# A whole-model kernel rewritten: small recorded operations, a list scheduler, shared buffer pools, attention in halves of the array

## The reference, cut to what matters

```python
for l in range(DEPTH):
    mod = silu_c @ w_mod[l] + b_mod[l]          # shift, scale, gate: two sets
    hx = modulate(rms_norm(x, norm1_g[l]), sh1, sc1)
    if l % 2 == 0:
        out_x, out_c = even_mixer(hx, hc, ...)   # pooling channels | attention, one output projection
    else:
        out_x = conformer_conv(hx, *conv_args)
    x = x + g1 * out_x
    x = x + g2 * sq_relu_mlp(modulate(rms_norm(x, norm2_g[l]), sh2, sc2), mlp_w1[l], mlp_w2[l])

# attention: 8 query heads, 2 key/value heads of 64; blocks of 128 queries see 256 context keys,
# a sink, and up to 3 blocks of 128 keys (|i - j| <= 128); one softmax over all of them
# conv: a = h @ w_pw1; g = a1 * sigmoid(a2); depthwise conv of width 31;
#       LayerNorm over channels; silu; @ w_pw2
```

## Time and profile before

| what | value |
|---|---|
| three runs | 3942.7, 3958.9, 4101.8 us (median 3958.9) |
| span of the slowest core in the profiled execution | 3916.7 us (all cores 3899.7 to 3916.7) |
| PE busy | 3255.1 us, 83% of the span |
| DVE, ACT, POOL busy | 1877.3, 1261.7, 273.3 us |
| transfers | 247.8 MB written, mean 63 GB/s |

### The profile page before, as it was taken

One profiled execution on the slowest core, in us unless ns is written; L12 is line 12 of the kernel. 1 busy time (PEld: TensorE's weight loads), 2 busy tenths in 40 slices (PEclk: granted clock), 3 DMA queues, 4 the chain that ended last, 5 costly groups with the idle time before them and its releaser, 6 DMA issues.

```text
span 3916.7 us, 44703 instructions; the slowest of 8 cores (3899.7 to 3916.7 us)
## 1 busy us (share of the span) xinstructions
PE 3255.1 (83%) x17961; PEld 1504.3 (38%) x18282; DVE 1877.3 (48%) x2895; ACT 1261.7 (32%) x1889; POOL 273.3 (7%) x287
## 2 busy tenths in 40 slices
PE   2477778999978877799996677789999687799997
PEld 1233334555533333455553233334444233244443
DVE  1233335565631245556663333346656223656666
ACT  4134443111143256211114434441112515621112
POOL 0000000000022000000003100000000400000000
PEclk8688889999988998899998788899999799899998
DMA  9932335544213532544321222235432146122212
GB/s 182 148 52 36 45 46 77 74 60 70 34 22 58 119 89 46 76 66 72 49 38 27 55 49 49 43 55 85 76 62 37 30 90 142 29 43 44 39 27 86
DMA packets 225888, 247.84 MB, mean 63 GB/s; under 512 B 15120, under 2 KB 196752, under 8 KB 225680
## 3 DMA queue, kind: packets, MB, share of 16 engines
q0 software_dynamic: 154160, 170.61, 29.4%
q1 hardware_dynamic: 71520, 74.36, 7.3%
HBM read 397.96 MB, written 17.56 MB: 106 GB/s over the span
## 4 chain that ended last, share of the span: by engine, by line
PE 64%; issue 15%; ACT 7%; DVE 6%; DMA 4%; POOL 2%; another core or an unknown queue 0%; SPq 0%; DVEq 0%; POOLq 0%; ACTq 0%
PE ps L143 64%; DVE ARENA L143 5%; ACT ARENA L143 3%; ACT H L143 3%; POOL TMP L143 2%; DMA ARENA<-w_mod 2%; DMA ARENA<-ropes 1%; DMA wr<-w_in 1%; DVE TMP L143 1%; ACT RST L143 1%; DMA ARENA<-gscr 0%; DVE X L143 0%; POOL ARENA L143 0%; ACT L143 0%
## 5 line engine op out<-in xcount | busy, mean ns | idle before, releaser
L143 PE MATMUL ps<-H,wr 128*128 128x512 bf16 (+1 forms) x6558 | 1432.0, 376 | 66.9 <-ACT ARENA L143 33.9
L143 PE MATMUL ps<-ARENA,wr 128*128 128x512 bf16 (+1 forms) x5085 | 1091.3, 371 | 69.7 <-DVE X L143 62.6
L143 ACT ACTIVATE ARENA<-ps 128x512 f32<-128x512 f32 (+2 forms) x1033 | 565.3, 583 | 1797.7 <-PE ps L143 1765.0
L143 DVE SCALAR_TENSOR_TENSOR X<-ps,MODV,X 128x512 f32<-128x512 f32 (+1 forms) x1296 | 905.7, 719 | 195.0 <-PE ps L143 123.4
L143 PEld LDWEIGHTS ps<-H,wr 128*128 128x128 bf16 x6704 | 665.9, 100 | 800.8 <-issue 73.5
L143 DVE TENSOR_TENSOR ARENA<-ARENA 128x512 bf16<-128x512 f32 (+4 forms) x849 | 527.6, 628 | 907.7 <-ACT ARENA L143 905.2
L143 PEld LDWEIGHTS ps<-ARENA,wr 128*128 128x128 bf16 x5184 | 508.0, 99 | 632.4 <-DVE X L143 84.7
L143 PE MATMUL ps<-ARENA 128*32 128x512 bf16 (+4 forms) x3389 | 419.9, 386 | 244.1 <-DVE ARENA L143 116.7
L143 DVE TENSOR_TENSOR ARENA<-ps,ARENA 128x512 bf16<-128x512 f32 (+5 forms) x300 | 197.5, 671 | 442.1 <-PE ps L143 350.2
L143 PEld LDWEIGHTS ps<-ARENA 128*32 128x32 bf16 (+2 forms) x3410 | 148.2, 102 | 498.3 <-ACT ARENA L143 137.2
L143 ACT ACTIVATE H<-TMP,AB 128x512 bf16<-128x512 f32 (+1 forms) x296 | 210.4, 727 | 106.2 <-POOL TMP L143 54.9
(11 more groups left out here) (41 smaller groups left out, 682.9 us busy)
## 6 DMA issues: line engine op xcount, KB each, us to landing
wr<-w POOLq DMA_DIRECT2D x64, 1024.0 KB, 9.3
ARENA<-w_mod POOLq DMA_DIRECT2D x48, 1024.0 KB, 14.7
ARENA<-gscr SPq DMA_DIRECT2D x256, 135.0 KB, 3.5
wr<-w_in POOLq DMA_DIRECT2D x18, 1024.0 KB, 10.2
wr<-w_out POOLq DMA_DIRECT2D x18, 1024.0 KB, 11.0
wr<-pw POOLq DMA_DIRECT2D x12, 1024.0 KB, 9.6
X<-xT SPq DMA_DIRECT2D x4, 2048.0 KB, 36.5
gscr<-ARENA SPq DMA_DIRECT2D x64, 128.0 KB, 1.7
```

The lines of the kernel that those rows point to most:

```text
L143: ins = getattr(e, it[1])(*it[2], **it[3])
```

## The change

The arithmetic is almost the same; the program around it is new.

- **Recording and scheduling.** Operations are now small objects (`Rec.add`) with an engine, a fixed cost, keys read and written, and virtual buffers. `Rec.schedule` then plays them forward in time and starts on each free engine the ready operation with the lowest number whose buffers fit. What comes out is still one fixed order per engine, made before the program runs. Waits that other waits imply are left out (`_emit_waits`).
- **Pools.** PSUM is a pool of 8 banks, weights a pool of 5 slabs (shared with the modulation slabs), and scratch tiles come from pools that all stages share. H is also the target for queries, attention and pooling outputs.
- **Order of tiles.** Context tile 4 first, then 0 to 3; the first mixer starts when tiles 4 and 0 have their norm and 4 modulation slabs are there. Layer 0's other slabs come later.
- **Attention** (`att`): the two groups' score matmuls go to two halves of the rows into two banks, with one Exp of 128x1024 and one mask for both; the products with V and with ones have 64 columns each and go to two halves of the columns; the denominator is handled for both groups at once. U is computed once per block, together with V.
- **Statistics.** Sums over channels use 32 columns of ones: four chunks go to four column groups of one bank; one more matmul with a constant matrix adds the groups up, after ACT and DVE have split the float32 sum into two bf16 parts (`norm`, `ln`).
- **Convolution.** Sigmoid is replaced by Tanh of half the argument with the factor 0.5 folded into a constant. The norm's multiplication runs on DVE, not on POOL.
- **Packed inputs.** The host lays out weights, X and the output so that each partition's row is contiguous.

```diff
-NSLOT = 4
+NSLOT = 5
...
+    def schedule(self):
...
+                    while h and n < 60:
+                        pr = heap_pop(h)
+                        o = ops[pr[1]]
...
+                        got = fits(o)
+                        if got is None:
+                            tried.append(pr)
+                            continue
+                        pick = (o, got)
+                        break
...
-                            MM(PS[sbk][:, :], KT[gs, m * 128:(m + 1) * 128], Qs[gs, :, nl * 128:(nl + 1) * 128], True, True,
-                               reads=KTk + Qk, writes=[psk(sbk)], last=True)
-                            ACT(P[:, :], PS[sbk][:, :], AF.Exp, [psk(sbk)], Pk, scale=0.125)
...
+                            return [(sc.ap[:, g * 512:(g + 1) * 512].rearrange("p (c q) -> p c q", c=4),
+                                     KT.ap[g * 64:(g + 1) * 64, m * 128:(m + 1) * 128],
+                                     H[t][g * 64:(g + 1) * 64, 0:4, nl * 128:(nl + 1) * 128],
+                                     True, True, [KT.k(m)] + hk(t)[0:4], sc.keys()) for g in range(2)]
...
+                        ACT("Exp", lambda sc=sc, P=P: (P.ap[:, :], sc.ap[:, :], {"scale": 0.125}), sc.keys(), P.keys(), 1024)
...
+                            for g in range(2):
+                                out.append((pnd.ap[g * 64:(g + 1) * 64, 0:512], V.ap[:, m * 128 + g * 64:m * 128 + (g + 1) * 64], P.ap[:, g * 512:(g + 1) * 512],
+                                            first, lst_, [V.k(m)] + P.keys(), pnd.keys()))
+                            for g in range(2):
+                                out.append((pnd.ap[g * 64:(g + 1) * 64, 512:1024], ONE1[:, :], P.ap[:, g * 512:(g + 1) * 512],
+                                            first, lst_, [("one1",)] + P.keys(), pnd.keys()))
...
-                for c in range(8):
-                    MM(PS[pb][:, 0:n], ONES[:, :], H[:, c, t0:t0 + n], c == 0, c == 7,
-                       reads=[("H", ti, c), ("c", "ones")], writes=[psk(pb)], last=(c == 7))
...
+                return [(pa.ap[32 * (c % 4):32 * (c % 4) + 32, 0:n], ONES[:, :], H[t][:, c, :], c < 4, c >= 4,
+                         [("H", t, c), ("ones",)], [pa.k(c % 4)]) for c in range(8)]
```

The sequence in which the mixer of an even layer is recorded, which sets the numbers that the scheduler goes by:

```diff
+            if upd:
+                rest(4)
+            att(0)
+            poolmix(0)
+            proj(2, True)
+            proj_out(wo, 0, l)
+            norm(0, l, 1)
+            att(1)
+            poolmix(1)
+            proj(3, True)
+            proj_out(wo, 1, l)
+            norm(1, l, 1)
+            rest(2)
+            rest(3)
```

More of the change, by code:

```diff
@@ L104, in op, with mm @@
         eng.q.append(("op", meth, args, kw or {}, eng.sem, 1))
+        eng.hist[eng.count] = dict(eng.seen)
         self._record(eng, eng.count, reads, writes)
-    def mm(self, out, lhsT, rhs, start, stop, reads=(), writes=(), last=True):
-        if self.dry:
-            return
+    def mm(self, out, lhsT, rhs, start, stop, reads, writes, last):
         eng = self.E["pe"]
@@ new lines, in DMA, with emit, slab @@
+        def DMA(q, chan, f, reads, writes, nbytes, cost=None, soft=(), bias=0):
+            def emit(Sd):
+                ch = chan() if callable(chan) else chan
+                Sd.dmas(q, Sd.chan(ch), f(), phys(reads), phys(writes))
+            return R.add(q, emit, reads, writes, cost if cost is not None else (1.0 if q == "pool" else 0.08), dma=nbytes, soft=soft, bias=bias)
+        MMC = 0.2157
+        def slab(src, cols=4096):
+            vb = VBuf(wpool, "w", 1, 1, "w")
+            DMA("pool", lambda: "w%d" % vb.slot, lambda: [(vb.ap[:, 0:cols], src)], [], vb.keys(), 128 * cols * 4)
+            return vb
@@ new lines, in poolmix @@
+                    ACT("Identity", lambda pp=pp, g4=g4: (H[t][:, g4, :], pp.ap[:, 0:n], {"scale": vec("pscale", i2 * 4 + g4, i2 * 4 + g4 + 1)}),
+                        pp.keys() + VK, [("H", t, g4)], n, 1)
+            proj(4, upd)
+            proj(0, True)
+            proj(1, True)
+            if pre is not None:
+                pre()
+            wo = [slab(w_out[i2 * 2]), slab(w_out[i2 * 2 + 1])]
+            if pre is not None:
+                for j in range(6, 12):
+                    mod_slab(0, j)
@@ new lines, in build, with pre0 @@
+        norm(4, 0, 0)
+        norm(0, 0, 0)
+        for t in (1, 2, 3):
+            load_x(t, [("modv", 0, 3)])
+            norm(t, 0, 0)
+        def pre0():
+            mod_slab(0, 4)
+            mod_slab(0, 5)
+        for l in range(DEPTH):
+            upd = l < 2
+            tiles = ORD if upd else ORD[1:]
+            if l % 2 == 0:
+                even_mixer(l, upd, pre0 if l == 0 else None)
+            else:
+                conv_mixer(l, tiles)
+            mlp(l, tiles, None)
@@ L979, in build @@
+        order, total, busy = R.schedule()
+        if info is not None:
+            info["order"] = order
+            info["total"] = total
+            info["busy"] = busy
+        Sd = Sched(nc, st)
+        for o in order:
+            for (vb, s_) in o.allocs:
+                vb.slot = s_
+                bind(Sd, vb)
+            o.emit(Sd)
+        for nm, ch in Sd.chans.items():
+            if nm[0] == "o":
+                Sd.E["sp"].q.append(("wait", ch.sem, ch.count))
         with nc.Block() as block:
-            Sreal.flush(block)
+            Sd.flush(block)
```

1681 lines of the change are left out of this document (978 added, 703 removed).

## The result

The changed kernel takes **3304.62 us** (median of 4 runs, 3265.87 to 3584.15) where the kernel before, on the same chip, took 4030.36 (3942.74 to 4422.25). In some runs of either kernel four or all eight cores show a lower clock than in the others and the time is longer, so the ratio is formed from the undisturbed runs (3265.87 and 3266.98 us of the changed kernel): **0.8286, 95% interval 0.8199 to 0.8374**. A second measurement on another chip gave 0.8321 (0.8305 to 0.8337). The forecast was 3195, with a range from 3070 to 3360.

A forecast was written before the change was run, and what follows sets the result against it. It took PE work (3035 us of a 3917 us span) plus 880 us of waiting and slow clock as the bound; 2853 + 20 + 62 + 112 + 71 + 20 + 22 = 3160 span, plus 35 gives 3195 us, range 3070 to 3360.

The forecast's parts named there:

- The count of work: PE's matmuls over the whole program, counted in units of 0.216 us: 3035 us before, 182 us less after, 2853 remaining.
- the clock was priced in attention only: Lower PE clock in attention's half-idle stretches: 1 us per block, 34 us for both layers.
- Convolution's waits: PE waiting in the convolution mixers: 7 us per tile for 8.5 tiles and 11 us at the borders, 71 us.
- Tile changes: 446 changes of tile shape on PE at 0.04 us each, taken as 20 us; upper end 96 us.
- The start: Time before the first mixer matmul: 10.7 MB to load at 173 GB/s, 62 us where 144 were spent; upper end 98.
- ACT over 75% busy in the even mixers: Expected sign in the attention layers: ACT limits there, over 75% busy, with about 1.02 us per Exp.
- The MLPs' ends: Waiting at the borders of all four MLPs: 20 us, where about 200 were lost before.
- The signs: Expected profile marks: clock 0.96 or more, first mixer matmul near 62 us, first MLP matmul near 353, MLP steps unchanged.
- the halves: Rival in attention: matmuls on two halves of the array don't run side by side; about 3265 us, chance 8%.
- the slots: Rival: five shared weight buffers come free late and slabs hold up PE; slower than before, up to 4440 us, chance 2%.
- Better packed than I think: Rival: projections fill attention and the clock stays up, mixer waits fall from 183 to 80; about 3080 us, chance 10%.
- The waits stay: Rival: mixers keep their share of waiting; only work, start and MLP ends are gained; about 3540 us, chance 10%.

The follow-up runs named there:

- The run without halves: Changed kernel with attention's matmuls no longer split over halves of the array (same rows for both groups' scores, 128 columns for values and ones): 3326.8 us at the lowest.
- the run with full statistics: Changed kernel with the norm's statistics by eight matmuls of full 128 columns instead of four column groups, a split and an adding matmul: 3286.19 us.
- The combination with four slots: Changed kernel with padding written late, eleven vectors in one transfer, norm pieces behind Exp and Silu, and four weight buffers instead of five: 3202.34 us median, ratio 0.8159.
- the combination: Changed kernel with padding written late, the eleven vectors in one transfer, and the second norm's pieces behind Exp and Silu: 3222.4 us at the lowest, ratio 0.8217.
- the run in recorded order: Changed kernel with each engine's operations in program order, not the scheduler's, and layer 0's twelve modulation slabs loaded at the start: 4162.35 us at the lowest.
- the packed vectors: Changed kernel with eleven small vectors in one transfer, the first modulation slab held back, and padding recorded later but still scheduled early: 3266.78 us, ratio 0.8323.
- the padding alone: Changed kernel with the zeros padding the convolution's scratch memory written only after layer 0's last modulation values: 3268.08 us at the lowest.

## Why the prediction was right, and where it was off

Against the profiled execution: span 3160 forecast, 3265.4 measured, 105 us short, and the forecast had 81 us too little busy time and 24 too little idle time. The 35 us that I put between the span and the median were right by chance (the median is 39 over the span, the fastest run 0.5).

| term | forecast | measured | from |
|---|---|---|---|
| PE busy | 2907 (2853 + 34 + 20) | 2988 | page |
| of it work at full speed | 2853 | 2837 | 13,151 units, a chunk at 1.73 |
| of it slow clock | 34 | 70 | half of the 139.5 us that PE was busy at 1.2 GHz |
| of it tile changes | 20 | 45 | 446 x 0.10 |
| of it ends before gaps | 0 | 34 | 204 gaps x (0.38 - 0.216) |
| PE idle at the start | 62 | 64 | 73.00 - 9.23 |
| idle in even mixers | 78 | 85 | 55.2 + 30.1 |
| idle in conv mixers | 71 | 110 | 58.4 + 51.5 |
| idle at MLP ends and the end | 42 | 18 | rows of the stages |

The granted clock was at its lower level for 209 us in all (3265.4 x (1 - 0.968) = 104 is half of that), but PE was idle in 70 of them. The last row is a matter of the profile: a matmul before a gap is shown 0.38 us long, one with another behind it takes 0.216.

- **The count of work held.** The matmuls in 73 to 408 us of after, each at its full-speed duration, are 228 us (forecast 231), and the MLPs of the first two layers take 510 and 512 us, eight steps of 63.98. The run without halves shows that their 480 units were really gone; the run with full statistics shows 24 of the 40 us of the norms. A chunk was priced 0.14 us too high, 10 us in all.
- **The step that failed: the clock was priced in attention only.** I gave 1 us to a block, 34 in all. At 1.2 GHz PE was busy for 68 us in the two even mixers and 69 in the two convolution mixers, half of which is lost: 34 us in the even mixers, as forecast, and 35 in convolution, where I priced none, though the earlier trace rows has 0.91 and 0.93 there. What a gap leaves behind is seen in one row: after 7.06 us of waiting, a chunk takes 3.60 us at a granted clock of 0.50 that takes 1.91 in the earlier trace rows.

```profile
1088.61 3.60 PE L155 MATMUL ps<-ARENA 128*32 128x512 bf16 x32 [7.06 <-DMA ARENA<-gscr]
```

- **Convolution's waits were 39 us too low.** I summed ACT's operations against PE's and found ACT at 34 us per tile. That balance leaves out what stands in a queue at the wrong time: the norm's eight pieces, and the chunk loads, for which PE waited 40.4 of the 80.4 us in this group's row:

```profile
L155 PE MATMUL ps<-ARENA 128*32 128x512 bf16 (+3 forms) x3044 | 251.1, 385 | 80.4 <-DMA ARENA<-gscr 40.4
```

In conv 1 the chunk loads took a median of 3.4 us and up to 13. The combination with four slots, made against these two causes, gave 30 us in conv 1 and 11 in conv 3.
- **Tile changes were 0.10 us, not 0.04.** The small remainder that I took from the earlier trace rows came of a chunk priced at 1.87 instead of 1.73 us. The drain of which the Trainium skill speaks (TensorEngine Tiling (Array Packing), Key Properties) fits the trace: 0.10 us at each change, half a matmul, between my two ends.
- **The start: 73 for 62, and for another reason.** I reckoned with bytes alone. The rows below are the start of after (PE's busy time, clock, DMA share, GB/s): the DMA engines are full for 48 us, and then move nothing from 56 to 68, since the next slabs wait for slots that the modulation matmuls hold, and these stand behind norms that came late. In the combination the engines are busy throughout, and it is 55 to 59.

```profile
0.00:48.00 48.00, 0.00 (x0) 1.00 0.96 178
52.00:56.00 4.00, 0.00 (x0) 1.00 0.48 76
56.00:60.00 4.00, 0.61 (x2) 1.00 0.02 2
60.00:64.00 4.00, 1.83 (x6) 1.00 0.00 0
64.00:68.00 4.00, 2.63 (x65) 1.00 0.00 0
```

- **ACT over 75% busy in the even mixers: wrong, and 85 for 78 us of idle time is partly luck.** ACT is busy for 197.11 of 322 us, 61%. The Exp costs what I said (1022 ns), but PE's own part was longer than my 3.2 us per block by slow clock and changes, and I forecast 26 waits of 3.0 us for ACT (by my own terms 6.4 - 3.2 = 3.2, which makes 83). What stands before the score matmuls in 73 to 408 us is far less (count, busy us, mean ns, idle before):

```profile
L155 PE MATMUL ps<-H,ARENA 64*128 64x512 bf16 x164 | 34.1, 434 | 10.3 <-ACT ARENA L155 7.5 <-DVE MODV L155 1.5 <-ACT H L155 0.6
```

In both layers some 31 us of the 85 were waits for an Exp, 10 of them before modulation matmuls. Some 13 were waits for the mask on DVE, which I had put among the work that costs nothing. The others stood before norms, projections and pooling.
- **The MLPs' ends cost nothing** where I gave 20, and the end 18 for 22.
- **The signs.** The mean clock is 0.968 (0.96 or more was forecast). The first MLP matmul comes near 408 us, not 353: 11 us from the start, and 280 us of PE's busy time in layer 0's mixer for 231.
- Of the rivals, the halves are refuted though their time was hit, and the slots are refuted. "Better packed than I think" did not come: the mixers kept 195 us of idle time, not 80. "The waits stay" at 3540 did not come either; the run in recorded order, at 4162, shows how large such waits can get.

## What to carry to other kernels

Once PE is over 90% busy, price each remaining gap twice: its length, and the matmuls behind it at 1.2 GHz; here the second came to some 70 us beside 277 of gaps. When a kernel is built by a list scheduler, look for work that is early because its engine was free, not because anybody waits for it: padding, prefetched slabs and a finished tile's norm each stood before something that PE wanted. Such locks hide one another, so open them together before you judge one worthless: the packed vectors gave nothing while the padding held the start, the padding alone nothing, both together 16 us at the first mixer matmul and 13 in the span.

## What the runs showed of the hardware

- Eleven small transfers of SP (0.5 to 96 KB) landed at 45 us beside software-queue slabs with rows of 8 KB or more, at 18 us beside slabs with rows of 2 KB, and as one transfer at 3.6 us beside the large rows (the combination).
- Two matmuls on the two row halves of the array, or on the two column halves, take the time of one: 0.22 us per pair against 0.43 with the same rows or the full width.
- A change of tile shape costs 0.09 to 0.12 us of PE, whether between full and rows of 64, between rows and columns of 64, or between full and columns of 32.
- SP needed 27.8 us to issue the three transfers of the padding, 256 KB in all, while the DMA engines were full at the start, and 5.7 to 8.4 us for the same three at 315 to 319 us (the runs with the padding late).
